# Four Strassen pairs instead of three in the gate and up units, with part of each pair's weight forms built by accumulating DMA loads

## The chip, the cores and the metric

The kernel runs on one NeuronCore of one Trainium2 chip. Its time is the device time of one execution, in microseconds (us). Before the change it is 2110.53 us, the median of three runs (2110.38 to 2111.59).

## The reference

A small decoder trunk over 256 tokens of width 2048 in float32: layer 0 mixes tokens by sparse attention, layer 1 by a short gated convolution, and each mixer is followed by a SwiGLU feed-forward part of hidden width 5632:

```
x = x + _dsa_mixer(_rmsnorm(x, attn_norm[0]), ...)
x = x + _swiglu(_rmsnorm(x, ffn_norm[0]), w_gate[0], w_up[0], w_down[0])
x = x + _shortconv_mixer(_rmsnorm(x, conv_norm[0]), ...)
x = x + _swiglu(_rmsnorm(x, ffn_norm[1]), w_gate[1], w_up[1], w_down[1])

def _swiglu(h, w_gate, w_up, w_down):
    return (jax.nn.silu(h @ w_gate) * (h @ w_up)) @ w_down
```

The weights are read once, some 400 MB, and the two feed-forward parts are most of the work.

## The kernel before, in words

**Precision.** Each float32 operand is split into a rounded high part and a low remainder (fp32r tiles), and a product is three matmuls: high by high, high by low, low by high (`product`, lines 767 to 769). Each is 128x128 by 128x512.

**Slots.** Weights arrive in slots of 128 rows by 1024 floats per partition, 512 KB each: two row tiles of 512 columns. SyncE loads slot n into one of eight `stage` buffers (L399) as soon as the low part of slot n-8 is made. ScalarE writes the high part `w_hi` (L986) into a ring of four, once TensorE has finished slot n-4; VectorE writes the low part `w_lo` (L1354), and TensorE then uses the slot. All engines go through the slots in program order.

**Units.** In the feed-forward part a unit makes 512 columns of the gate and of the up product, for 256 tokens, out of 16 slots: for each of eight pairs kp of row tiles, an even slot of the gate's weights and an odd slot of the up projection's. There are 11 units (`BLOCKS`) for each layer, then the down projection (two units of 44 slots), and in layer 1 a convolution of four units of 24 slots. Evictions of a unit (L1640, L1655, L1660, L1667, L1674) stand in the first slots of the next. At the second pair of every unit TensorE turns the hidden rows of the unit before by eight short transposes (L577), a regular mark in the trace.

**Plain and mixed pairs.** A plain pair is eight products (24 matmuls): two token halves by two sides (gate, up) by two row tiles. A mixed pair uses a Strassen-Winograd form: seven products (21 matmuls), from four forms of the activations (`sx`, made once for a layer), and from forms of the weights, which are made again for each pair. With B11 and B21 the two tiles of the even slot and B12 and B22 those of the odd one, VectorE makes four half-slot forms (`mix_weights`, L1686 to L1691): three into `t_raw`, and one written over B12 in the stage buffer, for which ScalarE's split of the odd slot waits (`t_first`). ScalarE and VectorE then split the three forms of `t_raw` (`mixed_high` L1219, `mixed_low` L1696). TensorE's `mixed_pair` uses both slots and then the forms. There is one buffer of each form, so that `mix_weights` waits until TensorE has used those of the pair before (`t_used`).

**Which pairs are mixed.** `MIXED_PAIRS = (2, 4, 6)` of eight in the gate and up units, two in the last; five of 22 in each unit of the down projection; 11 in the convolution. That is 95 in all.

**GpSimd** does two short multiplications for each head group in the attention (L1932, L1934) and nothing afterwards.

Of the kernel before, what the change touches and what calls it, by code (L numbers as in the profile page):

```python
# [29 lines left out]
F32R = mybir.dt.float32r  # L30
# [48 lines left out]
def trunk(nc, x, attn_w_in, attn_w_out, conv_w_in, conv_w_out, w_gate, w_up, w_down,  # L79
          gains, head_gains, conv_taps, tables, mats, bounds, out):  # L80
    with ExitStack() as ctx:
# [83 lines left out]
        sb("hs_but_six_tiles", [P, FT - 6, 2 * TOK], F32R, stack=tail_part)  # L165
        sx = sb("sx", [P, 3, 4, TOK], F32R, stack=tail_part)
        tail_part.close()
        conv_part = ExitStack()
# [47 lines left out]
        mixed_hi = sem("mixed_hi")  # L216
        t_step = sem("t_step")
        t_first = sem("t_first")
# [128 lines left out]
        MIXED_PAIRS = (2, 4, 6)  # L347
        LAST_MIXED = (2, 6)
        FORM_PLACE = {4: 0, 2: 1, 6: 2}
        MIXED_K = tuple(2 * kp for kp in MIXED_PAIRS)  # L350
# [16 lines left out]
        ALL_FFN_MIXED = (BLOCKS - 1) * FFN_MIXED + len(LAST_MIXED)  # L367
        LAYER_MIXED = ALL_FFN_MIXED + 2 * DN_MIXED + CONV_MIXED

        def mixed_of(i):  # L370
            return LAST_MIXED if isinstance(i, int) and i == BLOCKS - 1 else MIXED_PAIRS
# [119 lines left out]
        def _(pe):  # L491
# [281 lines left out]

            def x_mixed(kp, s, form):
                return sx[:, FORM_PLACE[kp], form, 0:P], sx[:, FORM_PLACE[kp], form, P:TOK]

# [23 lines left out]
            def mixed_pair(n, kp, mixed_pairs, count, operand, mixed_operand, bank_free):  # L800
# [40 lines left out]
            def ffn(layer, first, q):  # L841
# [9 lines left out]
                def body(i, first_time):  # L851
# [7 lines left out]
                    for kp in range(KT // 2):  # L859
                        if first_time and kp % 2 == 0:  # L860
                            pe.wait_ge(xs_ready, 4 * q + kp // 2 + 1)
                        if kp in mixed_of(i):
                            mixed_pair(n, kp, mixed_of(i), LAYER_MIXED * layer + FFN_MIXED * i, xs, x_mixed, bank_free)
# [8 lines left out]
                with pe.Fori(1, BLOCKS - 1) as i:  # L872
                    body(i, False)
                body(BLOCKS - 1, False)
# [46 lines left out]
            for i in range(CONV_UNITS):  # L921
# [14 lines left out]
                for kp in range(KT // 2):  # L936
                    if i == 0 and kp % 2 == 0:
                        pe.wait_ge(xs_ready, 4 * 2 + kp // 2 + 1)
                    if kp in CONV_PAIRS[i]:
# [4 lines left out]
                        mixed_pair(n, kp, CONV_PAIRS[i], conv_mixed(i), xs, x_mixed, bank_free)  # L944
# [29 lines left out]
        def _(act):  # L974
            def split(first, slots, per_loop=0, i=0, at=0, after_first=None):

                for j in range(at, at + slots):
                    n = first + per_loop * i + j

                    if after_first is not None:  # L980
                        act.wait_ge(t_first, after_first)
# [33 lines left out]
            def forms_high(q, j):  # L1015
# [3 lines left out]
                act.wait_ge(mixed_step, 4 * (FFN_MIXED * (q // 2) + max(j - 1, 0)))  # L1019
# [8 lines left out]
            def mixed_x_high(q, j):  # L1028

                act.wait_ge(mixed_step, 4 * (FFN_MIXED * (q // 2) + j))  # L1030
                nc.scalar.activation(sx[:, FORM_PLACE[MIXED_PAIRS[j - 1]], :, 0:P], mixed, ACT.Copy).then_inc(mixed_hi, 1)

# [151 lines left out]
            def norm_steps(q, j):  # L1184

                steps = {4: [lambda: res_square(q, j)], 6: [lambda: forms_high(q, j)]}
                if j:
                    steps = merged(steps, {7: [lambda: mixed_x_high(q, j)]})
# [7 lines left out]
            def take_p1(unit, n, mixed_pairs, count):  # L1196

                act.wait_ge(slot_used, n + 2 * mixed_pairs[-1] + 1)
                act.wait_ge(t_ready, count + len(mixed_pairs))
# [21 lines left out]
            def unit_slots(first, slots, mixed_pairs, count, steps, per_loop=0, i=0, between=None):  # L1221

                for j in range(slots):
                    s = mixed_pairs.index(j // 2) if j // 2 in mixed_pairs else None
                    split(first, 1, per_loop, i, j, None if s is None or j % 2 == 0 else count + s + 1)
                    if s is not None and j % 2:
                        if s == 0 and between is not None:
                            between()
                        mixed_high(count + s)
# [3 lines left out]
            def ffn(layer, first, q):  # L1233

                def unit_steps(i):
                    unit = LAYER_UNITS * layer + i
                    count = LAYER_MIXED * layer + FFN_MIXED * i
# [768 lines left out]
```

## Time and profile before

| | |
|---|---|
| median of three runs | 2110.53 us |
| the profiled execution's own time | 2111.59 us |
| its span, first to last instruction | 2109.8 us |
| TensorE (PE) busy | 2095.5 us (99%) |
| VectorE (DVE) busy | 1728.5 us (82%) |
| ScalarE (ACT) busy | 1179.4 us (56%) |
| GpSimd (POOL) busy | 15.4 us (1%) |
| TensorE's granted clock | 1.000 |
| moved by DMA | 401.63 MB, mean 190 GB/s |
| DMA engines, plain loads | 59.5% of the span |

The profile is of one execution of 2111.59 us, and the span leaves out 1.8 us before the first and behind the last instruction. Busy time counts how long an engine has an instruction; an engine that is busy for 99% is where time is to be had, the others matter where it waits for them.

### The profile page before, as it was taken

How to read it: one execution, taken by the hardware profiler on the slowest of the kernel's cores; microseconds unless marked ns; L12 is line 12 of the kernel's file. 1: busy time of each engine (PE TensorE's matmuls, PEld its weight loads, DVE VectorE, ACT ScalarE, POOL GpSimd, SP SyncE). 2: the span in 40 equal slices, each digit the busy share in tenths (PEclk: the TensorE clock that was granted, in tenths of full speed). 3: DMA queues.
4: the chain of work that ended last, by engine and by line, in shares of the span. 5: the costliest groups of instructions: out<-in, count | busy, mean ns of one | idle time of the engine just before them, and what ended most of it. 6: DMA issues, size and time to landing. Idle time of an engine off the chain costs nothing.

```text
span 2109.8 us, 27947 instructions
## 1 busy us (share of the span) xinstructions
PE 2095.5 (99%) x9741; PEld 1743.7 (83%) x9741; DVE 1728.5 (82%) x1965; ACT 1179.4 (56%) x1321; POOL 15.4 (1%) x14
## 2 busy tenths in 40 slices
PE   8999999999999999999999999999999999999999
PEld 7888878888888888888888888888888888888887
DVE  5887757999999997877788788569999999978776
ACT  5466555666566654554465555555666566545443
POOL 0001000000000000000000000000000000000000
PEclk9999999999999999999999999999999999999999
DMA  7545546666566656666666665566665666565664
GB/s 226 154 140 158 168 171 177 203 202 196 191 201 201 200 188 204 197 203 192 197 189 192 189 199 188 197 174 203 200 200 187 201 200 199 192 205 195 207 199 131
DMA packets 234765, 401.63 MB, mean 190 GB/s; under 512 B 15040, under 2 KB 56128, under 8 KB 234688
## 3 DMA queue, kind: packets, MB, share of 16 engines
q1 hardware_dynamic: 233824, 399.23, 59.5%
q10 hardware_dynamic: 864, 1.37, 0.2%
q8 instruction: 49, 0.80, 0.2%
q14 instruction: 28, 0.23, 0.0%
HBM read 398.45 MB, written 2.10 MB: 190 GB/s over the span
## 4 chain that ended last, share of the span: by engine, by line
PE 97%; DVE 2%; ACT 0%; issue 0%; DMA 0%; SPq 0%; ACTq 0%; DVEq 0%
PE ps L767 24%; PE ps L769 24%; PE ps L768 24%; PE ps L513 6%; PE ps L544 4%; PE ps L543 4%; PE ps L542 4%; PE ps L518 3%; PE ps L577 2%; DVE w_lo L1354 0%; PE ps L695 0%; PE ps L633 0%; PE ps L704 0%; PE ps L685 0%; DMA res<-in_x 0%
## 5 line engine op out<-in xcount | busy, mean ns | idle before, releaser
L986 ACT ACTIVATE w_hi<-stage 128x1024 fp32r<-128x1024 f32 x748 | 781.9, 1057 | 751.8 <-PE ps L769 342.6
L1354 DVE TENSOR_TENSOR w_lo<-stage,w_hi 128x1024 fp32r<-128x1024 f32 x748 | 893.5, 1221 | 220.1 <-ACT w_hi L986 213.9
L767 PE MATMUL ps<-w_hi,xs 128*128 128x512 f32 x1254 | 490.5, 391 | 0.8 <-DVE w_lo L1354 0.8
L769 PE MATMUL ps<-w_hi,xs 128*128 128x512 f32 x1254 | 488.3, 389 | 0.0
L768 PE MATMUL ps<-w_lo,xs 128*128 128x512 f32 x1254 | 487.9, 389 | 0.0
L769 PEld LDWEIGHTS ps<-w_hi,xs 128*128 128x128 f32 x1254 | 235.4, 188 | 49.2
L767 PEld LDWEIGHTS ps<-w_hi,xs 128*128 128x128 f32 x1254 | 235.4, 188 | 49.1 <-issue 1.2
L768 PEld LDWEIGHTS ps<-w_lo,xs 128*128 128x128 f32 x1254 | 235.6, 188 | 48.1
L767 PE MATMUL ps<-w_hi,hs 128*128 128x512 f32 x584 | 227.6, 390 | 0.0
L769 PE MATMUL ps<-w_hi,hs 128*128 128x512 f32 x584 | 227.2, 389 | 0.0
L768 PE MATMUL ps<-w_lo,hs 128*128 128x512 f32 x584 | 227.2, 389 | 0.0
L513 PE MATMUL ps<-xs,w_hi 128*128 128x512 f32 (+1 forms) x528 | 170.8, 406 | 0.0
L1696 DVE TENSOR_TENSOR t_lo<-t_raw,t_hi 128x1536 fp32r<-128x1536 f32 x95 | 166.7, 1755 | 3.4 <-ACT t_hi L1219 2.1
L1219 ACT ACTIVATE t_hi<-t_raw 128x1536 fp32r<-128x1536 f32 x95 | 140.9, 1483 | 16.8 <-DVE t_raw L1691 16.8
L767 PEld LDWEIGHTS ps<-w_hi,hs 128*128 128x128 f32 x584 | 109.6, 188 | 22.8
L769 PEld LDWEIGHTS ps<-w_hi,hs 128*128 128x128 f32 x584 | 109.6, 188 | 22.7
L768 PEld LDWEIGHTS ps<-w_lo,hs 128*128 128x128 f32 x584 | 109.7, 188 | 22.6
L518 PEld LDWEIGHTS ps<-xs,w_lo 128*128 128x128 f32 (+1 forms) x528 | 97.0, 188 | 21.4
L1686 DVE TENSOR_TENSOR t_raw<-stage 128x512 f32<-128x512 f32 x95 | 65.6, 690 | 57.1 <-PE ps L769 48.6
L518 PE MATMUL ps<-xs,w_lo 128*128 128x256 f32 (+1 forms) x528 | 103.4, 280 | 0.0
L542 PE MATMUL ps<-w_hi,hs 128*128 128x512 f32 x256 | 101.2, 395 | 0.0
L544 PE MATMUL ps<-w_hi,hs 128*128 128x512 f32 x256 | 99.7, 390 | 0.0
(209 smaller groups left out, 2482.0 us busy)
## 6 DMA issues: line engine op xcount, KB each, us to landing
stage<-in_w_gate SPq DMA_DIRECT2D x176, 512.0 KB, 3.8
stage<-in_w_up SPq DMA_DIRECT2D x176, 512.0 KB, 4.2
stage<-in_w_down SPq DMA_DIRECT2D x176, 512.0 KB, 4.5
stage<-in_conv_w_in SPq DMA_DIRECT2D x96, 512.0 KB, 4.4
stage<-in_attn_w_in SPq DMA_DIRECT2D x48, 512.0 KB, 3.9
stage<-in_attn_w_out SPq DMA_DIRECT2D x32, 512.0 KB, 5.0
stage<-in_conv_w_out SPq DMA_DIRECT2D x32, 512.0 KB, 4.9
stage<-in_attn_w_in SPq DMA_DIRECT2D x32, 256.0 KB, 3.3
```

The source lines that it names most:

```text
L513: return pe.matmul(ps[0:count, banks[m], :], w_hi[:, slot, at], rhs, start=k == 0, stop=last)
L518: return pe.matmul(ps[0:count, banks[m], TOK:], w_lo[:, slot, at], rhs[:, 0:TOK], start=False, stop=False)
L542: pe.matmul(bank, hi, w_hi[:, slot, cols], start=k == 0, stop=False)
L543: pe.matmul(bank, hi, w_lo[:, slot, cols], start=False, stop=False)
L544: mm = pe.matmul(bank, lo, w_hi[:, slot, cols], start=False, stop=k == tiles - 1)
L767: pe.matmul(ps[:, bank, :], hi, b_hi, start=start, stop=False)
L768: pe.matmul(ps[:, bank, :], hi, b_lo, start=False, stop=False)
L769: return pe.matmul(ps[:, bank, :], lo, b_hi, start=False, stop=stop)
L986: nc.scalar.activation(w_hi[:, j % RING, :], stage[:, at, :], ACT.Copy).then_inc(hi_done, 1)
L1219: nc.scalar.activation(t_hi[:, :, :], t_raw[:, :, :], ACT.Copy).then_inc(t_high, 1)
L1354: tt(w_lo[:, p, :], stage[:, stage_at(first + j), :], f32(w_hi[:, p, :]), ALU.subtract).then_inc(lo_done, 1)
L1696: tt(t_lo[:, :, :], t_raw[:, :, :], f32(t_hi[:, :, :]), ALU.subtract).then_inc(t_ready, 1)
```

## The change

The gate and up units mix four pairs, `(2, 3, 5, 6)`; the ninth counted from nought (`BLOCKS - 2`) mixes 2, 5 and 6, and the last one 2 and 5, because `sx` and the spare buffers overlie the last hidden tiles. The down projection and the convolution keep their pairs.

Every mixed pair of the whole kernel, those of the down projection and the convolution too, gets its weight forms in another way. GpSimd issues two accumulating DMA loads of 128x512 floats (256 KB) for it. The first adds B11 from memory onto B12 in the odd stage buffer, once that slot has landed. For the second ScalarE writes -B22 into a buffer `diff` (`negate`), and the load adds B12 from memory to it. VectorE then makes only two half-slot forms (`mix_weights`). The column sign of the second side is turned by this, which the evictions undo with a subtraction in place of an addition. High and low parts of the forms are made in two steps, `diff` first, then the other two, and TensorE's three products of the forms are put in that order (P7, P4, P6). In the feed-forward units pairs 3 and 6 have a `diff` buffer of their own. `negate` stands three slots ahead of the pair (`FFN_LEAD`), in the convolution two (`CONV_LEAD`).

```
-        MIXED_PAIRS = (2, 4, 6)
-        LAST_MIXED = (2, 6)
+        MIXED_PAIRS = (2, 3, 5, 6)
+        NINTH_MIXED = (2, 5, 6)
+        LAST_MIXED = (2, 5)
+        FFN_LEAD, CONV_LEAD = 3, 2
...
-                pe.wait_ge(t_ready, count + s + 1)
-                product(P6, mixed_operand(kp, s, 1), t_hi[:, 1, :], t_lo[:, 1, :], first, last)
-                product(P4, half(operand, k2, 1), t_hi[:, 2, :], t_lo[:, 2, :], False, False)
-                product(P7, mixed_operand(kp, s, 3), t_hi[:, 0, :], t_lo[:, 0, :], first, last).then_inc(t_used, 1)
+                pe.wait_ge(t_ready, 2 * (count + s) + 1)
+                product(P7, mixed_operand(kp, s, 3), t_hi[:, 2, :], t_lo[:, 2, :], first, last).then_inc(t_used, 1)
+                pe.wait_ge(t_ready, 2 * (count + s) + 2)
+                product(P4, half(operand, k2, 1), t_hi[:, 1, :], t_lo[:, 1, :], False, False)
+                product(P6, mixed_operand(kp, s, 1), t_hi[:, 0, :], t_lo[:, 0, :], first, last).then_inc(t_used, 1)
...
-                        act.wait_ge(t_first, after_first)
+                        act.wait_ge(u1_added, 16 * after_first)
...
+            def negate(first, i, kp, per_loop, count, diff, back):
+                at = stage_at(first + 2 * kp + 1)
+                act.wait_ge(loaded[at], landed(first + 2 * kp + 1, per_loop, i))
+                if not isinstance(count, int) or count >= back:
+                    act.wait_ge(t_ready, 2 * (count - back) + 1)
+                nc.scalar.activation(diff, stage[:, at, WIDE:], ACT.Copy, scale=-1.0).then_inc(negated, 1)
...
-            def mixed_high(count):
-                act.wait_ge(t_step, 3 * count + 3)
-                nc.scalar.activation(t_hi[:, :, :], t_raw[:, :, :], ACT.Copy).then_inc(t_high, 1)
+            def mixed_high(count, diff):
+                act.wait_ge(diff_added, 16 * (count + 1))
+                if not isinstance(count, int) or count:
+                    act.wait_ge(t_used, 2 * count - 1)
+                nc.scalar.activation(t_hi[:, 2, :], diff, ACT.Copy).then_inc(t_high, 1)
+                act.wait_ge(t_step, 2 * count + 2)
+                if not isinstance(count, int) or count:
+                    act.wait_ge(t_used, 2 * count)
+                nc.scalar.activation(t_hi[:, 0:2, :], t_raw[:, 0:2, :], ACT.Copy).then_inc(t_high, 1)
...
-            def mix_weights(first, i, j, count):
-                for jj in (j, j + 1):
-                    dve.wait_ge(loaded[stage_at(first + jj)], landed(first + jj, 16, i))
-                if not isinstance(count, int) or count:
-                    dve.wait_ge(t_used, count)
-                tt(t3, b22, b12, ALU.subtract).then_inc(t_step, 1)
-                tt(b12, b12, b11, ALU.subtract).then_inc(t_first, 1)
-                tt(t2, b22, b12, ALU.subtract).then_inc(t_step, 1)
-                tt(t4, b21, t2, ALU.subtract).then_inc(t_step, 1)
+            def mix_weights(first, i, j, count, diff):
+                dve.wait_ge(loaded[stage_at(first + j)], landed(first + j, 16, i))
+                dve.wait_ge(diff_added, 16 * (count + 1))
+                tt(t_raw[:, 0, :], b11, diff, ALU.add).then_inc(t_step, 1)
+                tt(t_raw[:, 1, :], b21, t_raw[:, 0, :], ALU.subtract).then_inc(t_step, 1)
...
+            def add_to(n, j, loop_slots, i, b11, b12, count, diff):
+                at = stage_at(n + j)
+                if not isinstance(count, int) or count:
+                    pool.wait_ge(u1_added, 16 * count)
+                pool.wait_ge(loaded[at], landed(n + j, loop_slots, i))
+                pool.dma_start(stage[:, at, 0:WIDE], b11, accum_op=ALU.add).then_inc(u1_added, 16)
+                if not isinstance(count, int) or count:
+                    pool.wait_ge(diff_added, 16 * count)
+                pool.wait_ge(negated, count + 1)
+                pool.dma_start(diff, b12, accum_op=ALU.add).then_inc(diff_added, 16)
```

How the order of instructions moves is seen at three places. VectorE in the last gate and up unit of layer 0, around pair 2 (L1354 is the low part of a slot), before:

```order
L1667 SCALAR_TENSOR_TENSOR total<-total,rs,gated 128x512 x2
L1686 TENSOR_TENSOR t_raw<-stage 128x512
L1687 TENSOR_TENSOR stage<-stage 128x512
L1689 TENSOR_TENSOR t_raw<-stage 128x512
L1691 TENSOR_TENSOR t_raw<-stage,t_raw 128x512
L1354 TENSOR_TENSOR w_lo<-stage,w_hi 128x1024 x2
L1674 TENSOR_TENSOR hs<-ps,hs 128x4x256
```

The same place now (L1733 is L1667 before, L1413 is L1354, L1740 is L1674):

```order
L1733 SCALAR_TENSOR_TENSOR total<-total,rs,gated 128x512 x2
L1750 TENSOR_TENSOR t_raw<-stage,t_raw 128x512
L1752 TENSOR_TENSOR t_raw<-stage,t_raw 128x512
L1413 TENSOR_TENSOR w_lo<-stage,w_hi 128x1024 x2
L1740 TENSOR_TENSOR hs<-ps,hs 128x4x256
L1757 TENSOR_TENSOR t_lo<-t_raw,t_hi 128x512
L1759 TENSOR_TENSOR t_lo<-t_raw,t_hi 128x1024
```

Four half-slot instructions have become two, which wait for the DMA, and the low part of the forms is two instructions.

ScalarE in the first gate and up unit of layer 0, slots 1 to 5 (L1018 is the high part of a slot, L986 before; L1254 is the new negation, L1261 and L1265 are the high parts of the forms):

```order
L1254 ACTIVATE t_raw<-stage 128x512
L1018 ACTIVATE w_hi<-stage 128x1024 x2
L1254 ACTIVATE diff_spare<-stage 128x512
L1018 ACTIVATE w_hi<-stage 128x1024 x2
L1036 ACTIVATE square,ss<-res 128x512 x2
L1018 ACTIVATE w_hi<-stage 128x1024
L1261 ACTIVATE t_hi<-t_raw 128x512
L1265 ACTIVATE t_hi<-t_raw 128x1024
```

The negation for pair 2 (slots 4 and 5) stands ahead of slot 1, and that for pair 3 ahead of slot 3.

GpSimd had nothing behind the attention's L1934; now its queue goes on with two loads for each mixed pair, here those of the first gate and up unit:

```order
L2012 DMA stage<-in_w_gate 128x512
L2016 DMA t_raw<-in_w_up 128x512
L2012 DMA stage<-in_w_gate 128x512
L2016 DMA diff_spare<-in_w_up 128x512
L2012 DMA stage<-in_w_gate 128x512
L2016 DMA t_raw<-in_w_up 128x512
L2012 DMA stage<-in_w_gate 128x512
L2016 DMA diff_spare<-in_w_up 128x512
```

The order is strict: a pair's second load waits for its negation, and the next pair's first load stands behind it.

## Rows read from the trace of the kernel before

**Rows 1.** The page, part 1: busy us (share of the span) xinstructions.

```profile
PE 2095.5 (99%) x9741; PEld 1743.7 (83%) x9741; DVE 1728.5 (82%) x1965; ACT 1179.4 (56%) x1321; POOL 15.4 (1%) x14
```

**Rows 2.** The page, part 4: the chain that ended last, by engine.

```profile
PE 97%; DVE 2%; ACT 0%; issue 0%; DMA 0%; SPq 0%; ACTq 0%; DVEq 0%
```

**Rows 3.** Chain in order of time: start us, us, what; the units' transposes.

```profile
443.13 0.88 PE ps L577 x8
485.54 0.87 PE ps L577 x8
...
782.25 0.87 PE ps L577 x8
825.34 0.87 PE ps L577 x8
```

**Rows 4.** Busy us (x instructions) by stretch; then clock, DMA share, GB/s.

```profile
443.13:485.54 42.41, 42.41 (x194) 35.19 (x192) 39.08 (x41) 25.98 (x25) 0.00 (x0) 1.00 0.60 198
...
782.25:825.34 43.09, 43.09 (x197) 35.76 (x195) 34.53 (x33) 22.14 (x22) 0.00 (x0) 1.00 0.62 198
1499.06:1541.44 42.38, 42.38 (x194) 35.18 (x192) 39.07 (x41) 25.98 (x25) 0.00 (x0) 1.00 0.60 198
1838.18:1881.24 43.06, 43.06 (x197) 35.74 (x195) 34.52 (x33) 22.13 (x22) 0.00 (x0) 1.00 0.62 198
```

**Rows 5.** VectorE's groups of 443.13 to 824: instruction, count, busy us, mean ns, idle.

```profile
L1354 DVE TENSOR_TENSOR w_lo<-stage,w_hi 128x1024 fp32r<-128x1024 f32 x146 | 172.3, 1219 | 7.3 <-ACT w_hi L986 6.3
L1696 DVE TENSOR_TENSOR t_lo<-t_raw,t_hi 128x1536 fp32r<-128x1536 f32 x26 | 45.6, 1754 | 0.3 <-ACT t_hi L1219 0.2
L1691 DVE TENSOR_TENSOR t_raw<-stage,t_raw 128x512 f32<-128x512 f32 x25 | 17.3, 693 | 0.8
...
L1686 DVE TENSOR_TENSOR t_raw<-stage 128x512 f32<-128x512 f32 x25 | 17.3, 692 | 20.3 <-PE ps L769 18.2 <-DVE total L1667 2.0
L1687 DVE TENSOR_TENSOR stage<-stage 128x512 f32<-128x512 f32 x25 | 17.1, 684 | 0.0
```

**Rows 6.** ScalarE's groups of 443.13 to 485.54.

```profile
L986 ACT ACTIVATE w_hi<-stage 128x1024 fp32r<-128x1024 f32 x16 | 16.7, 1056 | 14.4 <-DVE stage L1687 10.5 <-PE ps L769 3.7
L1219 ACT ACTIVATE t_hi<-t_raw 128x1536 fp32r<-128x1536 f32 x3 | 4.5, 1486 | 0.6 <-DVE t_raw L1691 0.6
...
L1200 ACT ACTIVATE gated<-ps 128x512 f32<-128x512 f32 x1 | 0.6, 574 | 0.0
```

**Rows 7.** DMA issues: transfer, queue, count, KB each, median us to landing.

```profile
stage<-in_w_up SPq DMA_DIRECT2D x176, 512.0 KB, 4.2
...
stage<-in_attn_w_in SPq DMA_DIRECT2D x32, 256.0 KB, 3.3
...
out<-res SPq DMA_DIRECT2D x2, 256.0 KB, 2.0
```

**Rows 8.** Line 399 from 485 to 1060 us: issues on SyncE's queue, and landing.

```profile
L399 SPq DMA_DIRECT2D stage<-in_w_up x58: 372/373/373, 487.8 to 789.7; - x58
...
DMA to landing us min/median/max: 3.5/4.1/6.6
```

**Rows 9.** GpSimd in order of time, from 250 us.

```profile
250.77 2.37 POOL L1934 TENSOR_TENSOR qr<-gated,tab 128x1024 f32<-128x1024 f32 x1 [10.94 <-ACT gated L1120]
```

**Rows 10.** The tile kr on VectorE: ns min/median/max, first and last start.

```profile
L1559 DVE TENSOR_TENSOR kr<-kr,k_sq x4: 615/1831/1833, 121.4 to 251.6; 128x256 f32<-128x256 f32 x4
L1562 DVE TENSOR_TENSOR kr<-kr,k_rt x4: 425/426/426, 122.1 to 253.5; 128x256 f32<-128x256 f32 x4
```

**Rows 11.** TensorE in order of time, 1055 to 1090 us: its one idle stretch there.

```profile
1087.09 0.47 PE L767 MATMUL ps<-w_hi,xs 128*128 128x512 f32 x1 [0.85 <-DVE w_lo L1354]
```

**Rows 12.** ScalarE in order of time, slot 10 of the convolution's first unit.

```profile
1075.71 1.05 ACT L986 ACTIVATE w_hi<-stage 128x1024 fp32r<-128x1024 f32 x1
```

**Rows 13.** VectorE in order of time, slot 12 of that unit.

```profile
1083.07 0.68 DVE L1686 TENSOR_TENSOR t_raw<-stage 128x512 f32<-128x512 f32 x1
```

More of the change, by code:

```diff
@@ L1270, in down @@
                 forms = {at: [lambda s=s: hidden_forms_high(layer, s)] for s, at in enumerate(FORM_SLOTS)}
-                unit_slots(first, FT, DN_PAIRS, count(0), merged(before, forms, {TAKE_SLOT: [take(0)]}))
+                diffs = same_diff(DN_PAIRS)
+                unit_slots(first, FT, DN_PAIRS, count(0), merged(before, forms, {TAKE_SLOT: [take(0)]}), diffs, FFN_LEAD)
                 unit_slots(first + FT, FT, DN_PAIRS, count(1),
-                           merged({TAKE_SLOT: [take(1)]}, {} if layer else two_norm_steps(0)))
+                           merged({TAKE_SLOT: [take(1)]}, {} if layer else two_norm_steps(0)), diffs, FFN_LEAD)
                 return merged(two_norm_steps(2), {9: [lambda: take_root(2)]})
@@ L1681, in mix_weights @@
                 if not isinstance(count, int) or count:
-                    dve.wait_ge(t_used, count)
-                b11, b21 = (stage[:, stage_at(first + j), k * WIDE:(k + 1) * WIDE] for k in range(2))
-                b12, b22 = (stage[:, stage_at(first + j + 1), k * WIDE:(k + 1) * WIDE] for k in range(2))
-                t3, t2, t4 = (t_raw[:, form, :] for form in range(3))
-                tt(t3, b22, b12, ALU.subtract).then_inc(t_step, 1)
-                tt(b12, b12, b11, ALU.subtract).then_inc(t_first, 1)
@@ L1688, in mix_weights @@
-                dve.wait_ge(t_first, count + 1)
-                tt(t2, b22, b12, ALU.subtract).then_inc(t_step, 1)
-                dve.wait_ge(t_step, 3 * count + 2)
-                tt(t4, b21, t2, ALU.subtract).then_inc(t_step, 1)
-            def mixed_low(count):
-                dve.wait_ge(t_high, count + 1)
-                tt(t_lo[:, :, :], t_raw[:, :, :], f32(t_hi[:, :, :]), ALU.subtract).then_inc(t_ready, 1)
-            def unit_slots(first, slots, mixed_pairs, count, steps, per_loop=0, i=0, ahead=None, between=None):
+                    dve.wait_ge(t_ready, 2 * count)
@@ L1700, in unit_slots @@
+            def unit_slots(first, slots, mixed_pairs, count, steps, diffs, per_loop=0, i=0, ahead=None, between=None):
                 for j in range(slots):
@@ L1704, in unit_slots @@
                             ahead()
-                        mix_weights(first, i, j, count + s)
+                        mix_weights(first, i, j, count + s, diffs[j // 2])
                     split(first, 1, per_loop, i, j)
@@ L1720, in unit_steps @@
                     at = ffn_evicts(layer, i)
[L1721 removed]
+                    return {0: [lambda: take_mixed(unit, LAYER_MIXED * layer + mixed_at(i) + len(mixed_of(i)), at),
                                 lambda: take_gate(n)],
@@ L1726, in unit @@
                 def unit(i, steps, ahead, between=None):
-                    unit_slots(first, 16, mixed_of(i), LAYER_MIXED * layer + FFN_MIXED * i, steps, 16, i, ahead, between)
+                    unit_slots(first, 16, mixed_of(i), LAYER_MIXED * layer + mixed_at(i), steps, ffn_diffs(i),
+                               16, i, ahead, between)
                 def later_unit(i):
@@ L1801, in down @@
                                {at + 1: [lambda s=s: mixed_hidden_low(layer, s)] for s, at in enumerate(FORM_SLOTS)})
-                unit_slots(first, FT, DN_PAIRS, done, merged(before, forms, takes(0)))
+                diffs = same_diff(DN_PAIRS)
+                unit_slots(first, FT, DN_PAIRS, done, merged(before, forms, takes(0)), diffs)
                 unit_slots(first + FT, FT, DN_PAIRS, done + DN_MIXED,
-                           merged(adds(0), {} if layer else norm(0), takes(1)))
+                           merged(adds(0), {} if layer else norm(0), takes(1)), diffs)
                 if layer == 0:
```

166 lines of the change are left out of this document (123 added, 43 removed).

## The prediction

> **What bounds the kernel now.** I read the page's busy shares first: TensorE is busy for 2095.5 of 2109.8 us, VectorE for 1728.5 [rows 1]. The chain of waits then says whether that busy time is also the path: TensorE holds 97% of it, VectorE 2% [rows 2]. So time goes with the number of matmuls, as long as the two engines that prepare weights keep ahead. Third, the chain in order of time, where each gate and up unit shows its eight transposes once: 42.41 us from one unit's to the next's, and 43.09 us at the end of a layer [rows 3]. Fourth, the table of stretches: in such a unit VectorE is busy for 39.08 of 42.41 us, ScalarE for 25.98, the DMA engines for 0.60, the clock is granted in full (1.00, the upper level) [rows 4]. VectorE is the second bound, with only 3.33 us of idle time in a unit.
>
> **What a mixed pair is worth on TensorE.** The stretch that ends layer 0's units holds the same 16 slots with two mixed pairs in place of three, and takes 43.09 in place of 42.41 us; in layer 1 it is 43.06 against 42.38 [rows 3, 4]. Both give 0.68 us for one pair. The same comes from the count: 42.41 less 0.88 for the transposes is 41.53 us for 183 matmuls (5 x 24 + 3 x 21), 0.227 each, and a mixed pair saves three. The change adds one pair in units 0 to 8 of each layer; units 9 and 10 keep three and two. That is 18 pairs, 54 matmuls: 18 x 0.68 = **12.2 us** less. TensorE's new order inside the pair has the same number of products. Nothing else on TensorE changes.
>
> **VectorE, in a unit with four pairs.** Removed for each of three pairs: four half-slot forms (692, 684, 692, 693 ns) and the low part of 1536 columns (1754 ns), 4.52 us, 13.5 in all [rows 5]. Added for each of four: two half-slot forms of 0.69, a 512-column low part that I take at the same 0.69, and a 1024-column one at the 1219 ns of L1354, 3.30 us, 13.2 in all. VectorE is then busy for 39.08 - 13.5 + 13.2 = 38.8 us of a unit of 42.41 - 0.68 = 41.73, and 3.0 us stay idle. The work lies closer, though. In slots 0 to 7 it has eight low parts (9.8), two pairs (6.6), evictions and the hidden rows' low part (some 7.9, ten instructions of 0.69 to 1.22), 24.3 us together, against 21.3 us on TensorE (48 matmuls of 0.227, transposes, 42 matmuls). It falls back by 3.0 us. The ring lets it be ahead by three slots (3 x 2.61 = 7.8 us) less one high and one low part (1.06 + 1.22), 5.5 us. So 2.5 us of cover are left there, slots 8 and 9 give 3.0 back, slots 10 to 13 take 2.0 again. I cost it at nothing; were the cover gone, every microsecond more would be one on TensorE.
>
> **ScalarE.** It loses three high parts of 1486 ns and gains for each of four pairs a negation (574 ns by the nearest copy), a high part of 512 columns (574) and one of 1024 (1056) [rows 6]: 25.98 - 4.5 + 8.8 = 30.3 of 41.73 us. Its wait of 10.5 us in a unit for the stage form that VectorE wrote (L1687) goes [rows 6]; what releases the odd slot is now the first load, made as soon as the slot has landed. Behind a late negation are queued the slot's high part and the other pairs' negations, behind the `t_hi` parts the next slots' high parts; all lie inside the 11 us of idle time.
>
> **The accumulating loads.** No row shows one, nor a DMA issued by GpSimd, so they are bounded. The path is: negation, GpSimd's issue, landing, then VectorE's two forms. `negate` stands three slots ahead of the pair: 7.8 us at the new pace of 2.61, less its own 0.57, leaves **7.2 us** for issue and landing. The issue costs 0.37 us on SyncE's queue [rows 8]; GpSimd's instruction in rows 9 takes 2.37. A landing takes 2.0 us for the 256 KB store and at most 6.6 for a 512 KB load [rows 7, 8]. So the sum is between 2.4 and 9.0 us. Nearest are the 256 KB loads with 3.3 us [rows 7]; with an issue midway, 1.4, I take 4.7 us: hidden, with 2.5 to spare. The first load of a pair (onto the odd stage slot) is easier, since a slot lands 4.2 us after its issue and is split many slots later. GpSimd's own time is 8 x 1.4 = 11 us of a unit, on an engine with nothing else to do; at 2.37 it is 19 us, still under 41.73.
>
> The Trainium skill ("DMA: Bandwidth & Descriptors", section "Anatomy of one DMA — SWDGE (gpsimd) path") fits a DMA of GpSimd with a fixed 2.0 us plus the bytes over 436 thousand a microsecond; my estimate from it is 2.6 us for 256 KB, which would leave the sum as it is. It gives no price for the accumulation, and no run shows one so far.
>
> DMA engines: 0.60 of 42.41 us is 25.4 us for 8 MB in a unit; eight loads of 256 KB are a quarter of that, 6.4 us, so 31.8 of 41.73 (0.76). Where reading the destination costs as much again it is 0.92; they become the bound only if an accumulated byte costs 2.6 plain ones.
>
> **Down projection, convolution, ends of layers.** Pairs as before, each with 4.52 - 3.30 = 1.2 us less on VectorE. In the down projection they are three pairs apart and the lead is three slots: nothing. In the convolution the lead is two slots, 5.4 - 0.57 = 4.9 us against my 4.7, and VectorE's lead in the ring covers a late load. At its start TensorE waits 0.85 us for VectorE [rows 11]. There the negation for pair 6 stands ahead of ScalarE's slot 10 at 1075.7 and the forms begin at 1083.1 [rows 12, 13], 7.4 us apart; freeing `diff` and the negation take some 1.2, so a load of 4.7 is in time, and VectorE's saving may take the 0.85 away. With a load of 9.0 it costs some 2 us. I take -0.4. The first unit of each layer gets a denser start (both pairs 2 and 3, one more set of activation forms); I give that +0.2 in all, between 0 and 2.
>
> **Sum.** 2111.59 (the profiled execution: span 2109.8 and 1.8 outside) - 12.2 - 0.4 + 0.2 = 2099.2. The profiled execution is 1.06 above the median of the runs, so the median should be **2098.1 us**.
>
> **Rival A: the loads come too late (slower).** The place is VectorE's wait for `diff` ahead of its two forms, with its own low parts and evictions queued behind. With a time T from the issue's start to landing the price is 4 x (T - 7.2) - 3.0 us for a four-pair unit, since VectorE has 3.0 to give; the change breaks even at T = 8.1. At the upper end, 9.0, it is 4.2 us in each of 18 units, 76, so 2098 + 76 = 2174 us. For it speaks that a DMA that reads, adds and writes has no row, and that landings vary from 3.5 to 6.6 under load; against it, that the middle is 4.1 for twice the bytes [rows 8]. Chance 0.09.
>
> **Rival B: GpSimd's issues hold VectorE up (slower, far).** While GpSimd multiplies from 250.77 to 253.14 us [rows 9], VectorE's kr<-kr,k_sq takes up to 1833 ns, against 615 at its shortest and 425 for the same shape in L1562 [rows 10]. The two engines can thus stop each other, for up to 1.4 us. If each issue did so, that is 8 x 1.4 = 11.2 us in a unit against 3.0 of idle time: 8.2 x 18 = 148, 2246 us; it decides from (3.0 + 0.68) / 8 = 0.46 us for an issue on. Against it: an issue is no read of large tiles. Chance 0.05. By the Trainium skill ("SBUF — State Buffer", section "Who interferes with whom") a VectorE instruction with two SBUF inputs shares its second read port with a GpSimd instruction that reads SBUF, and one waits out the other. The trace agrees with 1833 against 425 ns. That page infers that making descriptors needs the write port, which such VectorE instructions leave free; by that no term here changes.
>
> **Rival C: the gain stays away.** The dense slots 0 to 7 use up the 2.5 us of cover (short waits for semaphores, a load some 1 us late at pair 2 or 3), and TensorE waits 0.5 to 0.7 us in each unit: 18 x 0.6 = 11, about 2109 us. For it speaks that VectorE is already at 92% of a unit [rows 4]; against it, that its wait for TensorE's use of the forms (18.2 us at L1686 over nine units [rows 5]) falls away. Chance 0.07. That the change doesn't do what it says is hardly open, as the order shows the products and loads.
>
> **Chances and range.** The forecast has 0.79, spread from 2095 (the 0.85 and other short waits gone) to 2103 (the loads late here and there). A measurement of this kernel tells about 0.2% from no change, 4.2 us: faster means below 2106.3. Faster 0.79, the same 0.07 (rival C), slower 0.14 (A and B). The range, 2094 to 2107, holds the forecast and part of C; A and B lie outside.
>
> **What the profile afterwards would show.** 54 fewer matmuls, and 41.7 us between the transposes of neighbouring units; 41.0 or 42.4 would make the first term wrong. VectorE's groups: two half-slot forms of 0.69 with hardly any wait for a DMA ahead of them; a wait of more than 3 us in a unit speaks for A. Its 1024-column low parts at 1219 ns; longer ones beside GpSimd's issues speak for B. The accumulating loads landing in 3 to 6 us, DMA share 0.7 to 0.9. The 10.5 us of ScalarE's waits for L1687 gone. A time above 2107, or a unit above 42.2, makes the prediction wrong.

## The result, and the profile after

The changed kernel takes **2292.58 us** (median of four runs, 2284.55 to 2299.72), beside 2111.06 us for the kernel before: a ratio of 1.086 (95% interval 1.084 to 1.088), slower by 181.5 us. The forecast was 2098.1 us. The profiled execution took 2284.55 us. The page, part 1 (the columns of [rows 1]), and part 4 (those of [rows 2]), with the line of part 3 on GpSimd's queue:

```profile
PE 2147.2 (94%) x9687; PEld 1764.6 (77%) x9687; DVE 1669.6 (73%) x1952; ACT 1276.4 (56%) x1563; POOL 213.8 (9%) x240
...
q0 software_dynamic: 32544, 59.26, 16.3%
...
PE 52%; issue 31%; DMA 9%; DVE 5%; ACT 1%; POOL 1%; POOLq 0%; DVEq 0%; ACTq 0%; SPq 0%
```

The 54 matmuls are gone (9741 to 9687) and VectorE has 59 us less to do than before, but TensorE holds 52% of the chain in place of 97%. "Issue" is time in which an engine waited for nothing that the profile shows; nearly a third of the chain is of that kind. Whose it is, the waits from 400 to 860 us tell (engine, line, waited for: us in total, times, longest us):

```profile
POOL stage L2012 <- DMA stage<-in_w_up: 122.4, 10, 14.1
POOL t_raw L2016 <- issue: 81.0, 17, 6.9
...
POOL diff_spare L2016 <- issue: 72.2, 17, 5.2
DVE t_raw L1750 <- DMA diff_spare<-in_w_up: 63.1, 17, 5.3
...
PE ps L794 <- DVE w_lo L1413: 53.1, 18, 5.7
```

GpSimd's loads (L2012 a pair's first, L2016 its second) head the list. VectorE waits for the second one at its form (L1750), and TensorE for VectorE. GpSimd in order of time, the eight loads of one gate and up unit (start us, us, line, transfer, idle time before it and what ended that):

```profile
601.52 0.87 POOL L2012 DMA_DIRECT2D stage<-in_w_gate  x1 [11.75 <-DMA stage<-in_w_up]
607.23 0.88 POOL L2016 DMA_DIRECT2D t_raw<-in_w_up  x1 [4.84 <-issue]
612.41 0.88 POOL L2012 DMA_DIRECT2D stage<-in_w_gate  x1 [4.29 <-DMA t_raw<-in_w_up]
618.50 0.88 POOL L2016 DMA_DIRECT2D diff_spare<-in_w_up  x1 [5.21 <-issue]
623.23 0.87 POOL L2012 DMA_DIRECT2D stage<-in_w_gate  x1 [3.85 <-DMA diff_spare<-in_w_up]
627.79 0.88 POOL L2016 DMA_DIRECT2D t_raw<-in_w_up  x1 [3.69 <-issue]
634.26 0.87 POOL L2012 DMA_DIRECT2D stage<-in_w_gate  x1 [5.59 <-DMA t_raw<-in_w_up]
638.88 0.87 POOL L2016 DMA_DIRECT2D diff_spare<-in_w_up  x1 [3.75 <-issue]
```

An issue takes 0.88 us, and each next one starts 4.6 to 6.5 us after the one before, 5.34 as a mean (37.36 us for seven). Loads land 4.9 us (L2012) and 5.1 us (L2016) after their issue in the middle, so that there is no time in which two are under way. That is not the program's order: the second load of the first pair waits only for its negation, which ScalarE makes at 600.95 (ScalarE in order of time, same stretch), over 5 us before the issue at 607.23:

```profile
600.95 0.63 ACT L1254 ACTIVATE t_raw<-stage 128x512 f32<-128x512 f32 x1 [0.53 <-DMA stage<-in_w_up]
```

At the end of that row of loads stands VectorE, and behind it SyncE and TensorE (each in order of time):

```profile
644.88 0.69 DVE L1750 TENSOR_TENSOR t_raw<-stage,diff_spare 128x512 f32<-128x512 f32 x1 [5.35 <-DMA diff_spare<-in_w_up]
...
646.22 2.35 DVE L1413 TENSOR_TENSOR w_lo<-stage,w_hi 128x1024 fp32r<-128x1024 f32 x2
```

```profile
648.60 0.37 SPq L426 DMA_DIRECT2D stage<-in_w_up  x1
```

```profile
647.49 0.79 PE L794 MATMUL ps<-w_hi,xs 128*128 128x512 f32 x1 [5.72 <-DVE w_lo L1413]
```

And the row closes to a circle. The eighth load releases VectorE at 644.88, 43.4 us after the first was issued at 601.52. VectorE makes the two forms and the low parts of slots 12 and 13 until 648.6; only then is a stage buffer free for the next unit's slot 5 (SyncE at 648.60, eight slots on), and with its landing the next unit's first load is issued, at 653.84:

```profile
653.84 0.87 POOL L2012 DMA_DIRECT2D stage<-in_w_gate  x1 [14.09 <-DMA stage<-in_w_up]
```

That is 52.3 us for this round: 43.4 for the loads, 3.7 for VectorE, 5.2 for the slot. The 14.09 us that GpSimd waits here for a stage load are no lack of bandwidth but the way back through the ring.

The unit's length follows. Line L604, the transposes, from 350 to 900 us (ns min/median/max, first and last start), the set of unit 9 in order of time, and the stretch as a whole (columns of [rows 4]):

```profile
L604 PE MATMUL ps<-mat,total x80: 270/272/273, 408.2 to 866.5; 128*128 128x128 f32 x80
L604 PE MATMUL ps<-mat,res x8: 272/272/273, 357.3 to 358.0; 128*128 128x128 f32 x8
```

```profile
820.74 1.03 PE L604 MATMUL ps<-mat,total 128*128 128x128 f32 x8
```

```profile
400.00:860.00 460.00, 406.78 (x1707) 328.67 (x1707) 344.83 (x368) 265.62 (x302) 62.28 (x71) 0.94 0.75 204
```

From the first unit's set at 357.3 to unit 9's at 820.7 are nine intervals with four pairs, 51.5 us each, against 42.4 [rows 3]. They are 9.8 us over the forecast's 41.73, 88 us in this layer; with layer 1 (1499.0 to 1961.1, 51.3 each) it is 174 of the 185 us by which the profiled execution missed its own forecast of 2099.2. Unit 9, with three pairs, takes 45.0 us here and 45.4 in layer 1 in place of 42.4, some 6 us more. The DMA engines are busy for 0.75 of the time: not the bound. The clock is 0.94 as a mean, against 1.00 in [rows 4]; in parts of this stretch the lower level was granted, beside idle times of up to 5.7 us. Behind the idle time that ends at 647.49 the granted clock was 0.50 to 651.5, and the matmuls start 0.43 us apart in place of 0.23 (TensorE in order of time):

```profile
648.08 0.63 PE L795 MATMUL ps<-w_lo,xs 128*128 128x512 f32 x1
648.51 0.63 PE L796 MATMUL ps<-w_hi,xs 128*128 128x512 f32 x1
```

### The profile page after: what moved, and what is told of

Read it like the earlier page. It is cut to its first block, busy times and chain, and to the rows that moved or that the text cites. A ratio compares the mean times of both kernels' runs of the same rounds, so it can differ in the third digit from the quotient of the medians.

```text
span 2282.9 us, 29260 instructions
## 1 busy us (share of the span) xinstructions
PE 2147.2 (94%) x9687; PEld 1764.6 (77%) x9687; DVE 1669.6 (73%) x1952; ACT 1276.4 (56%) x1563; POOL 213.8 (9%) x240
## 3 DMA queue, kind: packets, MB, share of 16 engines
q0 software_dynamic: 32544, 59.26, 16.3%
## 4 chain that ended last, share of the span: by engine, by line
PE 52%; issue 31%; DMA 9%; DVE 5%; ACT 1%; POOL 1%; POOLq 0%; DVEq 0%; ACTq 0%; SPq 0%
PE ps L794 10%; PE ps L795 10%; PE ps L796 10%; PE ps L540 5%; DMA diff_spare<-in_w_up 4%; DMA stage<-in_w_up 4%; PE ps L571 3%; PE ps L569 3%; PE ps L570 3%; PE ps L545 3%; DVE w_lo L1413 3%; PE ps L604 1%; DVE t_raw L1750 1%; DMA t_raw<-in_w_down 1%; POOL stage L2012 0%
## 5 line engine op out<-in xcount | busy, mean ns | idle before, releaser
L1018 ACT ACTIVATE w_hi<-stage 128x1024 fp32r<-128x1024 f32 x748 | 780.1, 1054 | 551.7 <-PE ps L796 360.4
L1413 DVE TENSOR_TENSOR w_lo<-stage,w_hi 128x1024 fp32r<-128x1024 f32 x748 | 891.8, 1221 | 194.6 <-ACT w_hi L1018 189.8
L794 PE MATMUL ps<-w_hi,xs 128*128 128x512 f32 x1146 | 462.9, 404 | 116.5 <-DVE w_lo L1413 116.3
L796 PE MATMUL ps<-w_hi,xs 128*128 128x512 f32 x1146 | 457.0, 399 | 0.0
L795 PE MATMUL ps<-w_lo,xs 128*128 128x512 f32 x1146 | 455.9, 398 | 0.0
L794 PEld LDWEIGHTS ps<-w_hi,xs 128*128 128x128 f32 x1146 | 219.2, 191 | 178.3 <-DVE w_lo L1413 120.7
L796 PEld LDWEIGHTS ps<-w_hi,xs 128*128 128x128 f32 x1146 | 220.9, 193 | 47.5
L795 PEld LDWEIGHTS ps<-w_lo,xs 128*128 128x128 f32 x1146 | 220.4, 192 | 43.4
L794 PE MATMUL ps<-w_hi,hs 128*128 128x512 f32 x584 | 228.0, 390 | 4.7 <-DVE w_lo L1413 4.7
L796 PE MATMUL ps<-w_hi,hs 128*128 128x512 f32 x584 | 227.3, 389 | 0.0
L1750 DVE TENSOR_TENSOR t_raw<-stage,t_raw 128x512 f32<-128x512 f32 x75 | 51.9, 692 | 147.5 <-DMA t_raw<-in_w_up 66.6
L1265 ACT ACTIVATE t_hi<-t_raw 128x1024 fp32r<-128x1024 f32 x113 | 119.3, 1055 | 56.1 <-DVE t_raw L1752 52.2
L2012 POOL DMA_DIRECT2D stage<-in_w_gate x82 | 72.0, 878 | 761.2 <-DMA stage<-in_w_up 500.9
L1759 DVE TENSOR_TENSOR t_lo<-t_raw,t_hi 128x1024 fp32r<-128x1024 f32 x113 | 137.7, 1219 | 1.1 <-ACT t_hi L1265 1.1
L1750 DVE TENSOR_TENSOR t_raw<-stage,diff_spare 128x512 f32<-128x512 f32 x38 | 26.3, 693 | 139.7 <-DMA diff_spare<-in_w_up 139.7
```

The lines of the kernel that those rows point to most:

```text
L794: pe.matmul(ps[:, bank, :], hi, b_hi, start=start, stop=False)
L795: pe.matmul(ps[:, bank, :], hi, b_lo, start=False, stop=False)
L796: return pe.matmul(ps[:, bank, :], lo, b_hi, start=False, stop=stop)
L1018: nc.scalar.activation(w_hi[:, j % RING, :], stage[:, at, :], ACT.Copy).then_inc(hi_done, 1)
L1265: nc.scalar.activation(t_hi[:, 0:2, :], t_raw[:, 0:2, :], ACT.Copy).then_inc(t_high, 1)
L1413: tt(w_lo[:, p, :], stage[:, stage_at(first + j), :], f32(w_hi[:, p, :]), ALU.subtract).then_inc(lo_done, 1)
```

## The experiments

Five of the eight asked for the cause and two for what was left; one is a control. Six have a median of several runs with an interval; two are one execution each.

**The room for descriptors, 576 bytes in place of 512.** Theory R: what a partition keeps for the descriptors of GpSimd's DMAs holds one accumulating load at a time.

```
-    nc = bacc.Bacc("TRN2", ..., num_devices=1, dynamic_dma_scratch_size=512)
+    nc = bacc.Bacc("TRN2", ..., num_devices=1, dynamic_dma_scratch_size=576)
```

> The changed kernel with 576 in place of 512 bytes of each partition set aside for the descriptors of GpSimd's DMAs, nothing else. Theory R (room): at 512 bytes the descriptors of one accumulating load fill more than half of the room, so that the next load can't be issued before the last has landed, and 8 loads of 5 to 6 us one behind the other need 45 us of a 42 us unit; with 576 bytes two fit: GpSimd's loads of one pair start 1 to 2 us apart, VectorE's wait for diff falls under 2 us in a unit, time 2098 to 2120 us. Theory Q (queue): GpSimd always waits for the landing of its last load, whatever the room: loads stay 5 to 6 us apart, time 2280 to 2300 us. Theory S (the kernel's own semaphores, the negation above all): as under Q, no change.

2118.29 us (six runs), ratio to the kernel before 1.0035 (1.0023 to 1.0048): 174 us of the 181.5 are gone with 64 bytes. GpSimd in order of time:

```profile
533.62 0.86 POOL L2012 DMA_DIRECT2D stage<-in_w_gate  x1 [7.40 <-DMA stage<-in_w_up]
534.88 0.86 POOL L2016 DMA_DIRECT2D t_raw<-in_w_up  x1 [0.39 <-issue]
538.77 0.89 POOL L2012 DMA_DIRECT2D stage<-in_w_gate  x1 [3.03 <-DMA stage<-in_w_gate]
540.95 0.88 POOL L2016 DMA_DIRECT2D diff_spare<-in_w_up  x1 [1.28 <-ACT diff_spare L1254]
```

The second load now follows 1.26 us behind the first, so two are under way at once; what the third waits for is the first one's landing, which its own semaphore asks for. Second loads take 5.7 us to land (median, 400 to 860 us), against 5.1 with 512 bytes: a single load did not get faster, the row of them did. Busy time of TensorE bounds what share the clock had:

```profile
PE 2090.0 (99%) x9687; PEld 1730.5 (82%) x9687; DVE 1676.4 (79%) x1952; ACT 1270.2 (60%) x1563; POOL 213.9 (10%) x240
```

The same 9687 matmuls take 2090.0 us in place of 2147.2: 57 of the 166 us between the two spans (2282.9 and 2116.6) were longer busy time, and 109 were idle time of TensorE. The mean clock of the two executions is 0.972 and 1.000, and most of the 57 us is the lower level. Not all: a first matmul behind a wait takes longer at the upper level too (0.50 us at 625.70, in place of 0.39).

**Both loads plain, 512 bytes.** The accumulation, and with it the sums, are left out.

```
-                pool.dma_start(stage[:, at, 0:WIDE], b11, accum_op=ALU.add).then_inc(u1_added, 16)
+                pool.dma_start(stage[:, at, 0:WIDE], b11).then_inc(u1_added, 16)
-                pool.dma_start(diff, b12, accum_op=ALU.add).then_inc(diff_added, 16)
+                pool.dma_start(diff, b12).then_inc(diff_added, 16)
```

> The changed kernel with both loads of a pair made plain (they overwrite in place of adding, so the sums are left out of the computation), same queue, same sizes, same waits. Theory R: a plain load takes fewer descriptors, two or more fit into 512 bytes, GpSimd issues the second of a pair within 2 us of the first where its negation is done; time 2098 to 2120 us. Theory Q: loads stay one behind the other; if only the adding makes them long (5 us against 3 for a plain one), 8 x 3.5 = 28 us would fit into a unit and the time would still fall to about 2100, but the starts would be no closer than the landings.

2115.74 us (one execution). GpSimd in order of time:

```profile
535.59 0.54 POOL L2016 DMA_DIRECT2D t_raw<-in_w_up  x1 [3.79 <-ACT t_raw L1254]
536.86 0.54 POOL L2012 DMA_DIRECT2D stage<-in_w_gate  x1 [0.72 <-DMA stage<-in_w_up]
```

A plain issue takes 0.54 us, not 0.88, a load lands in 3.8 (L2012) and 4.1 us (L2016, medians), and two are under way at once in the same 512 bytes. So an accumulating load takes more of that room than a plain one of the same bytes. The page, part 3, shows more: GpSimd's queue here, and then in the accumulating kernel with 576 bytes (packets, MB, share of 16 engines):

```profile
q0 software_dynamic: 18080, 59.26, 9.1%
```

```profile
q0 software_dynamic: 32544, 59.26, 16.9%
```

Both kernels issue 226 such loads with the same 59.26 MB: 80 packets for each plain load and 144 for each accumulating one. The engines' time for them is 192 us (9.1% of 2114.1) and 358 us (16.9% of 2116.6), 1.9 times as much.

**Only the second load of each pair, 512 bytes.** The first load, with the sum it makes, and ScalarE's wait for it are left out.

```
-                        act.wait_ge(u1_added, 16 * after_first)
...
-                pool.wait_ge(loaded[at], landed(n + j, loop_slots, i))
-                pool.dma_start(stage[:, at, 0:WIDE], b11, accum_op=ALU.add).then_inc(u1_added, 16)
```

> The changed kernel without the first load of each pair and the wait for it (B11 is not added onto B12 in the stage buffer: that sum is left out of the computation). Four accumulating loads in a unit in place of eight. Theories R and Q alike: 4 x 6 = 24 us of loads fit into 42, and a diff load waits for no first load; T from issue to landing is 6 us, under the 7.2 that hide it: time 2098 to 2106 us. Theory L (each load is too slow by itself, more than 7.2 us from negation to landing): VectorE's waits for diff stay, time above 2150 us.

2117.88 us (one execution). GpSimd in order of time (L2010 is L2016 here):

```profile
541.46 0.87 POOL L2010 DMA_DIRECT2D diff_spare<-in_w_up  x1 [5.07 <-ACT diff_spare L1252]
```

The loads now wait for their negation alone. With four accumulating loads in a unit the room of one is enough: 4 x 5.3 us and the 9 us of the way back are 30, under 41.7. The price lay in their number, one behind the other. The time is above the 2098 to 2106 that I expected: the units take 42.7 us, as with 576 bytes, and the experiments further down take up that rest.

**Three pairs as before (2, 4, 6), forms by loads, 512 bytes.**

```
-        MIXED_PAIRS = (2, 3, 5, 6)
+        MIXED_PAIRS = (2, 4, 6)
...
-        LAST_MIXED = (2, 5)
+        LAST_MIXED = (2, 6)
```

> One part of the change alone: the weight forms by accumulating loads, with the 512 bytes of descriptor room of the changed kernel, but pairs 2, 4, 6 as before (2 and 6 in the last unit), pair 4 with the spare diff buffer. Theory R (loads one behind the other, 5.0 to 5.8 us from start to start): six loads take some 34 us of the 42.4 us unit, they just fit, but a pair's two loads and the next negation lie close: between no change (2111 us) and 1 us lost in a unit (2131 us). Theory F (every pair pays for its late second load, however many pairs there are: VectorE's waits of 3 to 5 us at each pair): above 2150 us.

2118.35 us (six runs), ratio 1.0043 (1.0027 to 1.006). The units keep the length before, 42.4 us (484.46 and 526.84 here). Six loads of 5.3 us and the way back of 9 are 41 us and just fit. The loads alone bring nothing and cost 7 us. (The edit also moves the buffers' bookkeeping to the new pairs.) TensorE's own waits say that nearly all of it is three waits:

```profile
PE ps L794 <- DVE w_lo L1413: 6.4, 3, 2.4
```

From the chain's mark at 824.61 to that at 941.48, the end of the units and the down projection, it is 116.87 us, against 114.45 before (825.34 to 939.79), so 2.4 of the 7 lie there. The other two waits, 4.3 us together, lie behind 1881 us, in layer 1's down projection. The down projection's loads, which I had put at nothing, so have a price of their own.

**Four pairs, all forms by VectorE, no loads.**

```
-                dve.wait_ge(diff_added, 16 * (count + 1))
...
+                tt(diff, b12, b22, ALU.subtract).then_inc(diff_added, 1)
+                tt(b12, b12, b11, ALU.add).then_inc(u1_added, 1)
+                dve.wait_ge(diff_added, count + 1)
```

> The other part alone: four mixed pairs (2, 3, 5, 6), but all weight forms made by VectorE in four half-slot instructions, no negation, no accumulating loads. 54 matmuls fewer than before. VectorE would be busy for 39.1 + 4.5 = 43.6 us of a unit whose matmuls take 41.73. Theory B (VectorE becomes the bound): a unit takes 43.8 to 44.5 us, 2135 to 2150 us. Theory M (VectorE's idle time can be squeezed and TensorE stays the bound): 2098 to 2112 us.

2145.13 us (four runs), ratio 1.0166 (1.015 to 1.0181). A stretch of 42.73 us (columns of [rows 4]):

```profile
529.17:571.90 42.73, 41.28 (x184) 33.26 (x183) 41.70 (x49) 26.02 (x29) 0.00 (x0) 1.00 0.60 196
```

VectorE is busy for 41.70 of 42.73 us: a fourth pair without the loads makes it the bound, and a unit takes 44.1 us (transposes at 447.85 and 491.95). So the loads are what makes four pairs possible, given room for two.

**ScalarE's loop over the units written out, with 576 bytes.** What was left: 2118.3 is 20 us over the forecast. In the 576-byte kernel the units took 42.7 us, and at their ends ScalarE and TensorE show (each in order of time):

```profile
551.21 0.63 ACT L1261 ACTIVATE t_hi<-diff_spare 128x512 fp32r<-128x512 f32 x1 [2.33 <-PE ps L796]
...
555.60 1.28 ACT L1018 ACT_TABLE_LOAD   x1
```

```profile
563.40 0.50 PE L794 MATMUL ps<-w_hi,xs 128*128 128x512 f32 x1 [0.67 <-DVE gated L1721]
```

A table load (ScalarE's ACT_TABLE_LOAD) of 1.28 us, at the loop's head, stands ahead of the first high part of a unit, just where ScalarE has been held up by TensorE's use of pair 5's forms. VectorE's evictions come later by it, and TensorE waits 0.67 us for a bank. There is a second table load in each pass, ahead of L1238 (561.12 to 562.40); behind it ScalarE still waits 0.97 us for VectorE, so it holds nothing up:

```profile
563.38 1.34 ACT L1238 ACTIVATE gated<-gated,rs 128x512 f32<-128x512 f32 x2 [0.97 <-DVE gated L1721]
```

```
-                with act.Fori(1, last - 1) as i:
+                for i in range(1, last - 1):
```

> The kernel with 576 bytes of descriptor room, whose ScalarE loop over the gate and up units 1 to 8 is written out, so that the activation table isn't loaded again twice in each unit (1.28 us each, one of them right ahead of slot 0's high part). With 576 bytes a unit takes 42.70 us in place of the 41.73 of its matmuls: TensorE waits for the eviction of the gate banks (L1721), which stands behind slot 0's low and high part; in unit 9, whose code stands outside the loop and loads no table, the wait isn't there (41.79). Theory T (the table load at the loop's head is what makes the eviction late): 16 units get 0.97 us back, 2118.3 - 15.5 = 2102.8 us, 2101 to 2105. Theory V (the evictions are late because ScalarE waits at slot 13 for TensorE to free the form buffers of the adjacent pair 5): nothing or a few tenths in a unit, 2112 to 2118 us.

2106.97 us (eleven runs), ratio 0.9981 (0.9972 to 0.999): already faster than the kernel before. Of ScalarE's table loads at L1018 three are left of 19, of those at L1238 two of 16, and the units take 41.8 us. I had expected 2102.8, from 16 units with 0.97 us each to gain. There were 14 such intervals, seven in each layer, with some 0.9 us each, and the first two of layer 0 gave 0.5. Of what is left over the forecast the largest part is in the first units of both layers, 43.7 us each, as in the 576-byte kernel (here layer 0's; transposes in the chain):

```profile
358.46 0.87 PE ps L604 x8
402.19 0.87 PE ps L604 x8
...
528.38 0.87 PE ps L604 x8
570.20 0.87 PE ps L604 x8
```

**Control: the kernel before, with the same loop written out.**

```
-                with act.Fori(1, last) as i:
+                for i in range(1, last):
```

> The kernel before, with ScalarE's loop over the gate and up units written out, and nothing else. It asks what of the 2107.0 us of the unrolled kernel with four pairs is due to the pairs. Theory T (the loop head's table loads delay a unit's end only where VectorE and ScalarE have been brought close to TensorE): the units before already take 42.4 us with hardly any wait of TensorE, so writing the loop out gives nothing: 2110.3 to 2111.3 us, units 42.37 to 42.41. Rival (the loop head costs something in any version): the units come out shorter by 0.2 to 0.6 us, 2101 to 2107 us, and then the gain of the four pairs is none.

2111.06 us (eleven runs), ratio 1.000 (0.9991 to 1.0009). So the loop written out is worth nothing by itself: the kernel before had the same 1.28 us at each head (21 table loads at L986, three with the loop written out), and its cover hid them. In the kernel with four pairs they were worth 11 us.

**The best version: three pairs (2, 5, 6) in each layer's first unit, with 576 bytes and the loop written out.** In the first unit the last activation forms are made too, and pairs 2 and 3 stand side by side with one pair of buffers for the split forms; VectorE there, in the kernel with the loop written out:

```profile
366.26 0.69 DVE L1757 TENSOR_TENSOR t_lo<-diff_spare,t_hi 128x512 fp32r<-128x512 f32 x1 [0.45 <-ACT t_hi L1261]
368.05 1.23 DVE L1759 TENSOR_TENSOR t_lo<-t_raw,t_hi 128x1024 fp32r<-128x1024 f32 x1 [1.10 <-ACT t_hi L1265]
```

```
+        FIRST_MIXED = (2, 5, 6)
...
-            last_two = {BLOCKS - 2: NINTH_MIXED, BLOCKS - 1: LAST_MIXED}
+            last_two = {0: FIRST_MIXED, BLOCKS - 2: NINTH_MIXED, BLOCKS - 1: LAST_MIXED}
```

> The unrolled kernel with 576 bytes (2107.0 us), but the first unit of each layer mixes 2, 5 and 6 only (pair 3's activation forms are still made there, for the units behind). Theory F (the first units' 2.0 us each over 41.73 come of pair 3 right behind pair 2 beside the last activation forms): a first unit takes 42.4 us, the pair less costs 0.68 us and 1.3 us come back, in each layer: 2104.4 us. Rival G (it is the activation forms of two more pairs that fill VectorE, not the weight forms): a first unit still has the wait of 0.8 us and takes 43.7 to 44.4 us: 2107 to 2108.3 us.

**2102.31 us** (five runs, 2100.54 to 2103.71), ratio 0.9958 (0.9945 to 0.9972): 8.6 us faster than the kernel before, and 4.7 faster than with four pairs everywhere, where 2.6 was expected. The chain (transposes) and the stretch of one unit with four pairs and one with two (columns of [rows 4]):

```profile
357.67 0.87 PE ps L607 x8
400.18 0.88 PE ps L607 x8
441.98 0.87 PE ps L607 x8
...
734.65 0.87 PE ps L607 x8
777.12 0.87 PE ps L607 x8
820.20 0.87 PE ps L607 x8
```

```profile
483.81:525.60 41.79, 41.79 (x190) 34.54 (x189) 38.50 (x42) 27.31 (x32) 7.07 (x8) 1.00 0.89 248
777.12:820.20 43.08, 43.08 (x196) 35.74 (x195) 32.53 (x32) 22.83 (x25) 1.76 (x2) 1.00 0.67 210
```

The first unit takes 42.5 us, as theory F had it, and the two after it 41.8 from the start, in place of 42.24 and 42.16 (the differences of the chain's marks at 402.19, 444.43 and 486.59 in the kernel ahead): the late start had been carried on, which F had not counted. In layer 1 that part is missing. The units of both layers are together 2.8 us shorter, near F's 2.6. Of the 4.9 us between the two profiled executions 1.3 lie in layer 0's down projection (116.2 and 114.9 us) and 0.8 ahead of the units, where the two kernels have the same program; no run explains these 2.1.

## Why the prediction was wrong

**The step that failed** is the accumulating loads. The prediction took the issue (1.4 us) and the landing (3.3) of one load as its cost, 4.7 us against 7.2 of cover, called a pair's first load the easier one, and gave GpSimd's own time as 8 x 1.4 = 11 us "on an engine with nothing else to do". The size of one load was only a little off: 0.88 us to issue, inside 4.9 to 5.7 from issue to landing, which the bounds of 2.4 to 9.0 held. What failed is that eight of them were taken to run beside each other. With 512 bytes each issue waits for the landing of the load before, though its own semaphores may be long met, so a unit has a row of eight, 5.3 us each. With the way back through the ring, 9 us, that is a round of 52, more than the unit's 41.7, and the units took 51.5. The kernel with 576 bytes shows it directly (one number changed, -174 us); plain loads and half as many loads show it from two sides, both with 512 bytes.

**Rival A** had the right place, VectorE's wait for `diff` with its low parts queued behind it, but a price by the length T of one load, at most 2174 us. No median of T was near 9 (the longest single landing was 7.9 us): a load was late because others stood ahead of it. The largest case I had written, 2246, was below the measured time; none of my rivals had the queue's room in it, and none had the clock: most of 57 us of the loss were the lower level, granted beside TensorE's idle times.

**Rival B** is false. With 512 bytes VectorE's low part takes 1220 ns in 146 instructions of 400 to 860 us, as in [rows 5], and a half-slot form 692; its groups there:

```profile
L1413 DVE TENSOR_TENSOR w_lo<-stage,w_hi 128x1024 fp32r<-128x1024 f32 x146 | 172.1, 1220 | 1.1
...
L1752 DVE TENSOR_TENSOR t_raw<-stage,t_raw 128x512 f32<-128x512 f32 x35 | 24.2, 692 | 1.2
```

GpSimd issued 71 loads in that stretch without one of them showing there. The port that the Trainium skill ("SBUF — State Buffer", section "Who interferes with whom") describes as shared lengthened VectorE's work beside GpSimd's multiplication in [rows 9, 10], and not beside its issues, which agrees with that page.

**Rival C** was real, once the loads had room: 42.7 us a unit, TensorE waiting 0.67 us, within the 0.5 to 0.7 I had given it. Its total of 2109 fell short of 2118.3, since the first units and the down projection cost more than I had given them. But I had costed it with hand-overs in general. The cause was one I had in the trace and left out, the table load of 1.28 us at the loop's head, and two further us at each first unit, where I took 0.2 in all.

**TensorE's 0.68 us for a pair** held in size: 43.08, 42.47 and 41.80 us for two, three and four pairs in the best version, 0.61 and 0.67 apart. Its 16 additional pairs are so worth some 10 us, and 8.6 came. **VectorE's** 38.8 us in a unit were 38.50, the work of the forms as reckoned (692, 684, 1219 ns). **ScalarE's** 30.3 were 29.8 with the table loads and 27.3 without. The DMA share was 0.89, near the 0.92 that I had given for a destination that costs as much again. **The convolution's start** was right in kind: in the best version TensorE waits for a low part 0.3 us in all, and the 0.85 us [rows 11] are gone. In size it was 1.15 us (473.34 us between the chain's marks around it, against 474.49 before), where I took 0.4. **The down projection** I put at nothing. Layer 0's takes 114.45 us before and 114.46 with plain loads, but 116.65 with 576 bytes and 114.92 in the best version, so accumulating loads cost 0.5 to 2.2 us there.

By the Trainium skill ("DMA: Bandwidth & Descriptors", section "Anatomy of one DMA — SWDGE (gpsimd) path") my estimate for 256 KB was 2.6 us; an accumulating load landed in 4.9 to 5.7 (medians of the stretch). Here the measurement decides.

What stays open: how many bytes one accumulating load takes of the room. 512 held one and 576 two, so if the whole room can be filled it is more than 256 and at most 288. Whether a third in flight would help wasn't tried.

## What to carry to other kernels

Cost a series of DMAs of one queue as a row first, number times the time from issue to landing, and only then as work that overlaps; what lets it overlap is a resource of its own, the room for descriptors, and here 64 bytes of it decided over 174 us. When a change uses up the cover of an engine, look for fixed costs that the cover had hidden (here a table load at a loop's head): they cost nothing before and most of their length after (0.9 of 1.28 us in a unit). Where an added piece pays in steady state, leave it out of the one unit that has other extra work: three pairs there were better than four.

## What the runs showed of the hardware

- An accumulating DMA load of 128x512 floats costs GpSimd 0.88 us to issue and lands in 4.9 to 5.7 us (medians from 400 to 860 us); a plain one costs 0.54 and lands in 3.8 to 4.1.
- 226 of them took 1.9 times the DMA engines' time of 226 plain ones (358 and 192 us), in 144 packets each against 80.
- With 512 bytes of dynamic descriptor room in a partition one accumulating load is in flight, with 576 two; plain ones overlap in 512. An issue that waits for room shows in the trace as a wait for "issue" (a pair's second load) or for the landing of the load before (a first one), with no semaphore of its own behind it.
- Beside idle times of up to 5.7 us, spread over the units, the mean granted clock was 0.94 (400 to 860 us), and TensorE's busy time grew by 57 us in the whole, most of it by the clock.
- In this program ScalarE loads a table twice in every pass of its loop, 1.28 us each, at the head and ahead of the silu; with the passes written out the loads at these two lines fell from 19 to 3 and from 16 to 2.
